# Two softmax groups' query and key slabs in a wide product shape, with the copies, sums and gate halves around them reordered

## The reference, cut to what matters

```python
q, k = rotary(heads(bq), pos, 32, theta), rotary(heads(bk), pos, 32, theta)  # only dims 0..31 of 128 are turned
p = softmax(where(causal, q @ k.T * d**-0.5, -inf))
ob = p @ v                                                                   # one block of 256 keys
y  = concat([oa, ob]) * silu(z)                                              # then y @ w_out, added to x
```

## Time and profile before

| | us |
|---|---|
| median of 3 runs | 584.1 (583.99 to 584.66) |
| the profiled execution's own time | 583.72 |
| span of its profile, first to last instruction | 581.9 |
| TensorE busy | 573.0 |
| VectorE busy | 429.8 |
| ScalarE busy | 390.3 |
| GpSimd busy | 72.2 |
| mean granted TensorE clock | 0.997 of full |

### The profile page before, as it was taken

One profiled execution on the slowest core, in us unless ns is written; L12 is line 12 of the kernel. 1 busy time (PEld: TensorE's weight loads), 2 busy tenths in 40 slices (PEclk: granted clock), 3 DMA queues, 4 the chain that ended last, 5 costly groups with the idle time before them and its releaser, 6 DMA issues.

```text
span 581.9 us, 9021 instructions
## 1 busy us (share of the span) xinstructions
PE 573.0 (98%) x3484; PEld 511.7 (88%) x3484; DVE 429.8 (74%) x672; ACT 390.3 (67%) x597; POOL 72.2 (12%) x77
## 2 busy tenths in 40 slices
PE   8999999999999999999999999999999999999995
PEld 7999989899899888888888889999889988888984
DVE  6879689677756874567766885799998974876663
ACT  6864784578458575657666847969759837566764
POOL 4130005036401000100000001102110200100002
PEclk9999999999999999999999999999999999999998
DMA  9756356456814833565345545326644563356201
GB/s 296 252 179 229 109 180 198 166 159 175 244 76 156 279 145 144 181 222 177 144 145 166 196 153 193 121 114 216 217 148 145 172 236 133 117 212 228 98 1 73
DMA packets 51854, 98.84 MB, mean 170 GB/s; under 512 B 1732, under 2 KB 7140, under 8 KB 51812
## 3 DMA queue, kind: packets, MB, share of 16 engines
q1 hardware_dynamic: 50628, 96.95, 49.1%
q0 software_dynamic: 1024, 1.05, 0.7%
q10 hardware_dynamic: 160, 0.27, 0.1%
HBM read 96.16 MB, written 1.05 MB: 167 GB/s over the span
## 4 chain that ended last, share of the span: by engine, by line
PE 97%; DVE 1%; ACT 1%; DMA 1%; issue 0%; DVEq 0%; SPq 0%; ACTq 0%
PE proj L1917 13%; PE proj L1941 10%; PE proj L1942 10%; PE proj L1943 10%; PE proj L1900 9%; PE proj L1902 9%; PE proj L1901 9%; PE proj L1918 7%; PE head L2157 4%; PE proj L1922 2%; PE head L2342 1%; PE head L2235 1%; PE proj L1921 1%; PE head L2001 1%; DMA x_residual<-in_x_dram 1%; PE head L2134 1%
## 5 line engine op out<-in xcount | busy, mean ns | idle before, releaser
L1146 DVE TENSOR_TENSOR w_lo<-raw_weights,w_hi 128x1024 fp32r<-128x1024 f32 x174 | 223.6, 1298 | 95.0 <-ACT w_hi L538 92.3
L538 ACT ACTIVATE w_hi<-raw_weights 128x1024 fp32r<-128x1024 f32 x174 | 182.3, 1056 | 111.5 <-PE proj L1943 49.1
L1900 PE MATMUL proj<-xT,w_hi 128*128 128x256 f32 x432 | 123.9, 287 | 0.0
L1902 PE MATMUL proj<-xT,w_lo 128*128 128x256 f32 x432 | 122.3, 283 | 0.0
L1901 PE MATMUL proj<-xT,w_hi 128*128 128x256 f32 x432 | 122.2, 283 | 0.0
L1917 PE MATMUL proj<-xT,w_hi 128*128 128x512 f32 x280 | 101.5, 402 | 0.0
L1900 PEld LDWEIGHTS proj<-xT,w_hi 128*128 128x128 f32 x432 | 82.8, 192 | 0.8 <-DVEq L1198 0.4
L1901 PEld LDWEIGHTS proj<-xT,w_hi 128*128 128x128 f32 x432 | 82.8, 192 | 0.4
L1902 PEld LDWEIGHTS proj<-xT,w_lo 128*128 128x128 f32 x432 | 82.8, 192 | 0.0
L1918 PE MATMUL proj<-xT,w_lo 128*128 128x256 f32 x280 | 78.4, 280 | 0.0
L1941 PE MATMUL proj<-w_hi,y 128*128 128x512 f32 x176 | 69.4, 395 | 0.0
(11 more groups left out here) (319 smaller groups left out, 888.2 us busy)
## 6 DMA issues: line engine op xcount, KB each, us to landing
raw_weights<-in_ev_w_in_dram SPq DMA_DIRECT2D x15, 2048.0 KB, 9.2
raw_weights<-in_od_w_in_dram SPq DMA_DIRECT2D x12, 2048.0 KB, 8.1
raw_weights<-in_ev_w_out_dram SPq DMA_DIRECT2D x4, 2048.0 KB, 7.8
raw_weights<-in_xa_wkv_dram SPq DMA_DIRECT2D x4, 2048.0 KB, 8.3
raw_weights<-in_od_w_out_dram SPq DMA_DIRECT2D x4, 2048.0 KB, 7.7
raw_weights<-in_xa_wq_dram SPq DMA_DIRECT2D x2, 2048.0 KB, 9.0
raw_weights<-in_xa_wo_dram SPq DMA_DIRECT2D x2, 2048.0 KB, 8.0
x_residual<-in_x_dram SPq DMA_DIRECT2D x2, 512.0 KB, 3.8
```

The source lines that it names most:

```text
L538: act.activation(ring_quarter(w_hi, n, q), raw_quarter(n, q), ACT.Copy).then_inc(hi_ready, 1)
L1146: dve.tensor_tensor(ring_quarter(w_lo, n, q), raw_quarter(n, q), ring_quarter(w_hi, n, q).bitcast(F32), ALU.subtract).then_inc(lo_ready, 1)
L1900: pe.matmul(dst, wh[:, k, :], x_hi[:, k, :], start=(k == 0), stop=False)
L1902: last = pe.matmul(dst, wl[:, k, :], x_hi[:, k, :], start=False, stop=(k == KC - 1))
```

## The change

Group B's q and k slabs (four slabs, sixteen quarters) become X. Each half slab is copied by ScalarE from the left halves of its pair of banks (`halves_copied`), the right halves are added by VectorE, which then frees the pair (`sum_rows`), and ScalarE copies the 32 turned rows from the sum (`packed_rows`). In g = 1 ScalarE's `turned_probs` for group 0 stand behind `ahead(q, 0)` and the copy of the gate's second half (`z_half`) instead of ahead of both. In the opening ScalarE scales the last half of the rows and VectorE takes over its 256 columns of the first `w_hi` quarter (so 512 in all). In `first_cross` VectorE does the fourth `query_summed` before `ahead(nv, 0)`.

```diff
-    SLABS += [("B", "q", "F", _g), ("B", "k", "F", _g), ("B", "v", "T", _g), ("B", "z", "X", _g)]
+    SLABS += [("B", "q", "X", _g), ("B", "k", "X", _g), ("B", "v", "T", _g), ("B", "z", "X", _g)]
...
+        def row_cols(rows, t, c):
+            return rows[:, t, :].rearrange("p (a c w) -> p a c w", a=2, c=2)[:, :, c, :]
...
(ScalarE, opening)
-            act.wait_ge(first_landed[0], 16)
-            act.activation(ring_quarter(w_hi, 0, 0)[:, 0:2, :], raw_quarter(0, 0)[:, 0:2, :], ACT.Copy).then_inc(first_hi, 1)
+            act.wait_ge(row_factored, 2)
+            act.activation(row_cols(mem_rows, 1, 1), row_cols(x_sb, 1, 1), ACT.Copy, scale=st[:, 7:8]).then_inc(rows_shared, 1)
...
(ScalarE)
-            def turn_rows_packed(n, u, w, s):
-                filled(act, n, u)
-                if w == 0 and u == 0:
-                    act.wait_ge(k_ready, SLABS[n][3])
-                for h in range(2):
-                    a = 64 * u + 32 * h
-                    act.activation(packed[a:a + 32, 2 * w, :], bank(n, u)[0:32, S * h:S * h + S], ACT.Copy)
-                copy_bank(n, u, W[:, w, 512 * u:512 * u + 512], s)
+            def halves_copied(n, half, w, s):
+                filled(act, n, 1, half)
+                act.activation(blocks(w)[:, 2 * half:2 * half + 2, :], bank_halves(n, half, 0), ACT.Copy).then_inc(s, 1)
+
+            def packed_rows(g, half, w, summed, s):
+                act.wait_ge(summed, 2 * g + half + 1)
+                if g and w == 0 and half == 0:
+                    act.wait_ge(k_ready, 1)
+                for h in (2 * half, 2 * half + 1):
+                    last = act.activation(packed[32 * h:32 * h + 32, 2 * w, :], blocks(w)[0:32, h, :], ACT.Copy)
+                last.then_inc(s, 1)
...
(ScalarE, stage_b)
                 z_half(before, 1)
+                if g:
+                    for h in range(4):
+                        turned_probs(h + 1, h, 384)
                 silu(before)
                 ahead(q, 1)
                 ahead(q, 2)
-                turn_rows_packed(q, 0, 0, q_rows)
+                halves_copied(q, 0, 0, q_halves)
                 ahead(q, 3)
                 if g:
                     y_high(2)
+                packed_rows(g, 0, 0, q_summed, q_rows)
                 ahead(k, 0)
-                turn_rows_packed(q, 1, 0, q_rows)
+                halves_copied(q, 1, 0, q_halves)
                 ahead(k, 1)
                 if g == 0:
                     act.preload_act_table_set("natural_log_exp_and_others")
                     rstd_a(1)
+                packed_rows(g, 1, 0, q_summed, q_rows)
                 ahead(k, 2)
-                turn_rows_packed(k, 0, 1, k_rows)
+                halves_copied(k, 0, 1, k_halves)
                 ahead(k, 3)
                 if g == 0:
                     y_high(1)
+                packed_rows(g, 0, 1, k_summed, k_rows)
                 ahead(v, 0)
-                turn_rows_packed(k, 1, 1, k_rows)
+                halves_copied(k, 1, 1, k_halves)
                 ahead(v, 1)
+                packed_rows(g, 1, 1, k_summed, k_rows)
...
(VectorE, opening)
             row_half(1, 0)
-            row_half(1, 1)
             dve.wait_ge(first_landed[0], 16)
-            dve.tensor_copy(ring_quarter(w_hi, 0, 0)[:, 2:4, :], raw_quarter(0, 0)[:, 2:4, :]).then_inc(first_hi, 1)
+            dve.tensor_copy(ring_quarter(w_hi, 0, 0)[:, 0:4, :], raw_quarter(0, 0)[:, 0:4, :]).then_inc(first_hi, 1)
...
(VectorE)
+            def sum_rows(n, half, w, copied, summed):
+                dve.wait_ge(copied, 2 * SLABS[n][3] + half + 1)
+                rows = blocks(w)[:, 2 * half:2 * half + 2, :]
+                dve.tensor_tensor(rows, bank_halves(n, half, 1), rows, ALU.add).then_inc(summed, 1)
+                halves_freed(n, half)
...
(VectorE, stage_b)
+                sum_rows(q, 0, 0, q_halves, q_summed)
                 ahead(q, 3)
                 if g == 0:
                     mem_turned(1)
-                if g:
+                else:
                     gated_b(0)
                 ahead(k, 0)
+                sum_rows(q, 1, 0, q_halves, q_summed)
                 ahead(k, 1)
                 if g == 0:
                     gated_a(1)
                 ahead(k, 2)
+                sum_rows(k, 0, 1, k_halves, k_summed)
                 rope_moba(0, q_rows, q_ready, 2 * g + 2, k, 3)
                 ahead(v, 0)
-                rope_moba(1, k_rows, k_ready, 2 * g + 2, v, 1)
-                ahead(v, 2)
+                sum_rows(k, 1, 1, k_halves, k_summed)
+                ahead(v, 1)
+                rope_moba(1, k_rows, k_ready, 2 * g + 2, v, 2)
...
(VectorE, first_cross)
+                query_summed(nq, 3)
                 ahead(nv, 0)
-                query_summed(nq, 3)
...
(TensorE, stage_b: q and k)
-                    slab_f(q, [0])
+                    slab_x(q, [0])
```

More of the change, by code:

```diff
@@ L190, in hybrid_trunk @@
         row_normed = sem("row_normed")
+        row_factored = sem("row_factored")
+        rows_shared = sem("rows_shared")
         sumsq = sem("sumsq")
@@ L229, in hybrid_trunk @@
         o_rstd = sem("o_rstd")
+        q_halves = sem("q_halves_copied")
+        q_summed = sem("q_summed")
+        k_halves = sem("k_halves_copied")
+        k_summed = sem("k_summed")
         kx_copied = sem("kx_copied")
@@ L417, in _ @@
             pool.drain().then_inc(first_hi_end, 1)
-            pool.wait_ge(first_hi, 2)
+            pool.wait_ge(first_hi, 1)
             pool.tensor_tensor(ring_quarter(w_lo, 0, 0), raw_quarter(0, 0), ring_quarter(w_hi, 0, 0).bitcast(F32),
@@ L921, in _ @@
             stage_b(0)
-            for h in range(4):
-                turned_probs(h + 1, h, 384)
             stage_b(1)
@@ L1225, in row_factor @@
                 dve.reciprocal(st[:, 6 + t:7 + t], st[:, 4 + t:5 + t])
-                dve.drain()
+                dve.drain().then_inc(row_factored, 1)
             def row_half(t, c):
-                cols = "p (a c w) -> p a c w"
-                dve.tensor_scalar(mem_rows[:, t, :].rearrange(cols, a=2, c=2)[:, :, c, :],
-                                  x_sb[:, t, :].rearrange(cols, a=2, c=2)[:, :, c, :], st[:, 6 + t:7 + t], None,
+                dve.tensor_scalar(row_cols(mem_rows, t, c), row_cols(x_sb, t, c), st[:, 6 + t:7 + t], None,
                                   ALU.mult).then_inc(row_normed, 1)
@@ L2032, in _ @@
             tile_turned(1, 1)
-            pe.wait_ge(row_normed, 4)
+            pe.wait_ge(rows_shared, 1)
             tile_turned(1, 2)
@@ L2039, in first_quarter_products @@
                 take_bank(n, 0)
-                pe.wait_ge(first_hi, 2)
+                pe.wait_ge(first_hi, 1)
                 dst = bank(n, 0)[:, 0:S]
@@ L2181, in stage_b @@
                 if g == 0:
-                    slab_f(q, [0])
+                    slab_x(q, [0])
                     mean_square_a(1)
-                    slab_f(q, [1, 2, 3])
-                    slab_f(k)
+                    slab_x(q, [1, 2, 3])
+                    slab_x(k)
                     slab_t(v)
                 else:
-                    slab_f(q, [0, 1])
+                    slab_x(q, [0, 1])
                     turn_probs_b(0)
-                    slab_f(q, [2])
+                    slab_x(q, [2])
                     out_b(0)
-                    slab_f(q, [3])
-                    slab_f(k)
+                    slab_x(q, [3])
+                    slab_x(k)
                     slab_t(v)
```

## The result

The changed kernel takes 585.87 us (median of 22 runs, 585.24 to 588.51), the kernel before 584.07 beside it (22 runs, 583.78 to 586.97). The ratio is 1.0029, 95% interval 1.0021 to 1.0036: slower by 1.8 us, about 0.3%. The profiled execution took 585.87, with a span of 584.0 (before 583.72 and 581.9), both at a mean granted clock of 0.997, so the 2.1 us between the spans are no matter of the clock.

A forecast was written before the change was run, and what follows sets the result against it. TensorE, busy 573.0 of 581.9 us, bounds the kernel. Terms -0.96 + 1.5 + 1.25 - 0.55 + 0 = +1.24, rounded to +1.3, give 585.0 from 583.72; the median, 0.4 higher, 585.4 us, range 582.9 to 586.5.

The forecast's parts named there:

- both waits: TensorE waits for late bank releases at group 0's v start, 1.5 us, and group 1's k third quarter, 1.25 us.
- The likeliest case: Both late bank releases in q and k slabs happen as worked out; 584.6 to 586.2 us, chance 0.55.
- Wide quarters: Group B's q and k: sixteen quarters at 2.82 us instead of 2.88 save 0.96 us, bounds 0.8 to 1.1.
- the rival built on it: In q and k an X quarter costs 2.86, saving only 0.32: 586.0 us; chance 0.11 shared with the cascade.
- Group 0, 1.5: At v's start TensorE waits 1.44 us for the sum of k's first half; 1.5 lost with reloading, bounds 0 to 1.8.
- The four steps of the walk: Group 0, before v: ScalarE's exponential, then VectorE's gated_a(1), low part and sum, freeing the pair at 140.45.
- Group 1, 1.25: At k's third quarter TensorE waits for the sum of q's second half; 1.25 us lost, bounds 0.5 to 1.8.
- The moved sum, -0.55: First cross attention: the fourth score starts earlier and runs shorter, saving 0.55 us, bounds 0.3 to 0.65.
- The opening, 0: Scaling half the last rows on ScalarE, beside the chain, changes nothing: 0 us, bounds 0.15 either way.
- The other six halves: Of eight q and k half slabs, six have their bank pairs free 1 us or more before wanted.
- the cascade of the rivals: VectorE later in v makes the keys' rotation late for the scores, 1 us more: 586.5; chance 0.11 shared with less saved.
- Banks free in time: At group 0's v and group 1's k third quarter the sums come early enough: 582.6 us, faster, chance 0.12.

The follow-up runs named there:

- The run with GpSimd late: Changed kernel with GpSimd's low part of y in group 1 held until VectorE's low part of k's fourth quarter is done; 585.13 us.
- the run with the keys' sum first: Changed kernel with VectorE's sum of k's first half moved ahead of ahead(k, 2), in both groups; 585.63 us.
- the fastest kernel of this study: Changed kernel with group 0's q and k back in F and old order, group 1 wide with early q copy and sum, k sum before its low part; 582.92 us.

## Why the prediction was right, and where a term was off

- **Slower, by both waits.** Forecast +1.3 and 585.4, measured +1.8 and 585.87. The likeliest case is the one that happened, at the two places named and by the releases named.
- **Wide quarters, -0.96.** Right: 14.11 for five is 2.82 each, against 2.88. By the formula of the Trainium skill (TensorE: Matmul & The Clock Gate; section Back-to-back issue gap), which that page gives for a product by itself, eight quarters in group 1 would as an estimate have given 0.16, where a wide quarter is 0.06 shorter and eight make 0.48. The formula does not carry over to this stream, and the rival built on it is out.
- **Group 0, 1.5.** Right: 1.50, a wait of 1.40 against 1.44 worked out. The four steps of the walk (exponential, `gated_a(1)`, low part, sum) are in the profile in that order.
- **Group 1, 1.25.** This is the term that was mis-sized: the place and the chain are right, the loss is 1.61. Read from where the turned probabilities start, y_high came 11.26 later (171.52 to 182.78) and not the 10.85 of the walk: I gave each `sum_rows` its 0.68, but the next operation begins 0.92 after its start, drain and issue included, and one lies there: 0.24 of the 0.41. About 0.16 more is ScalarE's table load, which began 2.18 after the turning (173.70), behind the end of the copies, where the walk had it at 2.02. The packed rows of the query took 0.83 to 0.85 for both and not 0.74. On the other side the low part was held for 0.49 (1.72 against 1.23), where my walk held it for 0.75: ScalarE was late too and met less of GpSimd. Together 0.41 + 0.10 - 0.26 = 0.25, and with the restart of 0.1 that I had set aside the 1.25 becomes 1.6. The run with GpSimd late shows the hold by itself. That the term is only 0.36 off is in part luck: a walk 0.51 short and a hold 0.26 too long stood against each other.
- **The moved sum, -0.55.** Right: -0.57 as read from the traces, in the changed kernel and alone; the median alone (-0.53) is inside its noise.
- **The opening, 0.** Right where the weights land as in the kernel before (q of group 0 at 115.44 to 115.59 against 115.48); the ratio alone, 1.0000, is too wide to show it. What I did not see is that GpSimd's copy can land on VectorE's row half, worth 0.48 in this execution, with either opening.
- **The other six halves.** None is late. The margin of the scores was called about 1 us; it is 0.9 (keys ready 153.91, scores at 154.80). It is what the run with the keys' sum first ran into: the cascade of the rivals is real, 0.28 of wait and not the 1 us of the rival, only not in the changed kernel.
- **Banks free in time.** My rival at 582.6 needed the releases early. In group 1 an order exists that does it and costs nothing (1.8 us back); in group 0 I tried one, and its gain is given back within 15 us.
- **The sum.** -0.96 + 1.50 + 1.61 - 0.57 = +1.58 with the opening at 0, where the medians have +1.8. The ratio's interval is +1.2 to +2.1 us, so the 0.2 left over can't be told from nothing.

## What to carry to other kernels

When a result needs a second engine before its bank can be given back, write down for each bank who releases it, behind what in that engine's list, and when it is wanted: eight products fewer are worth 0.06 us, one late release 1.5. A strict order makes an engine with a quarter of its time idle a full one: here VectorE sat idle for 2.48 us right ahead of the work that made a sum late. If a release is late, try to put its two steps ahead of the work that hangs on a third engine; where the list behind has no slack left, keep the older shape there and take the new one only where the order allows it, as the fastest kernel of this study does.

## What the runs showed of the hardware

A GpSimd copy that started 0.03 us behind a VectorE scaling with one SBUF tile as input stretched that from under 0.5 to 0.91 us, while the copy took 0.61; where the copy began in the middle of such a scaling (7.89 in the kernel before) two halves took 0.88 and the copy was stretched, to 0.81, and with it VectorE's own copy of 256 columns behind (0.70, where it takes 0.28 with the sum alone). And where GpSimd's copy began 0.01 to 0.03 behind a VectorE copy of 512 columns, in seven profiles, GpSimd's took 0.86 or 0.87 and VectorE's 0.42 or 0.43. So neither the number of inputs nor which started first tells by itself who is held; I had thought of a hold only for VectorE operations with two inputs, and of the later one as the one held. A 128x512 sum of 0.68 costs its engine 0.92: the code puts a drain behind it, and the next operation begins 0.24 after its end. And the first 512 KB of weights landed anywhere from 7.4 to 9.5 us in the profiled executions, with TensorE's wait for xT 1.42 and 1.59 in the two late ones where it is 0.60 otherwise, so half a microsecond in an opening can't be judged by one profile.
